# An expert stage in units of two 64-row sub-blocks on raw float32 weights, in place of 128-row blocks on weights split in two

## The reference

```python
def swiglu(h, wg, wu, wd):
    return (jax.nn.silu(h @ wg) * (h @ wu)) @ wd
...
        xs = hp[tok]
        y = swiglu(xs, w_gate_e[e], w_up_e[e], w_down_e[e])
        return (y.astype(jnp.float32) * rw[:, None]).astype(hf.dtype)
```

## Time and profile before

| | |
|---|---|
| median of three runs | 3558.13 us |
| lowest, highest | 3545.75, 3561.34 us |
| span of the profiled execution, first to last instruction | 3472.9 us |
| the profiled execution's own time | not shown; its span is 85.2 us under the median |
| PE, DVE, ACT, POOL busy | 85%, 62%, 49%, 27% of the span |
| mean granted clock of TensorE | 0.935 of full speed |
| moved by DMA | 730.08 MB, mean 210 GB/s |

### The profile page before, as it was taken

How to read it: one execution, slowest core, us unless ns; L and a number is a source line. 1 busy time by engine, 2 the same in 40 slices (tenths; PEclk the granted TensorE clock), 3 DMA queues, 4 the chain that set the end, 5 groups by cost and what they waited for, 6 DMA issues and landing times.

```text
span 3472.9 us, 61999 instructions
## 1 busy us (share of the span) xinstructions
PE 2951.9 (85%) x13151; PEld 2180.6 (63%) x13152; DVE 2164.1 (62%) x3443; ACT 1706.3 (49%) x2435; POOL 925.5 (27%) x794
## 2 busy tenths in 40 slices
PE   6699999999469989888798888888888888998883
PEld 2355555555358877776676767676767667776662
DVE  1146666666643665667676766666766675667774
ACT  0133333333133654656565655556556565656565
POOL 0001111111223333232333333333332323333331
PEclk9899999999779999999899999999999999999896
DMA  9501111111175887989998999899989998899997
GB/s 368 163 25 49 49 48 36 49 36 43 67 182 122 239 228 208 269 260 259 289 295 252 290 281 274 258 271 285 288 259 265 265 293 232 247 266 280 294 275 249
DMA packets 415300, 730.08 MB, mean 210 GB/s; under 512 B 31521, under 2 KB 297377, under 8 KB 414754
## 3 DMA queue, kind: packets, MB, share of 16 engines
q1 hardware_dynamic: 341314, 500.17, 42.5%
q0 software_dynamic: 73824, 228.47, 28.6%
HBM read 587.37 MB, written 141.19 MB: 210 GB/s over the span
## 4 chain that ended last, share of the span: by engine, by line
DMA 45%; PE 22%; issue 12%; DVE 8%; POOL 7%; POOLq 4%; ACT 2%; DVEq 0%; SPq 0%; ACTq 0%
DMA rec<-rec_tab 42%; PE PB L986 8%; POOL arena L461 3%; POOL acc_tab L492 3%; POOLq L476 3%; PE PB L951 2%; PE PB L1068 2%; PE PB L1070 2%; PE PB L1069 2%; DMA arena<-in_ada_b 1%; PE PB L1045 1%; PE PB L956 1%; DMA acc_tab<-arena,rec 1%; PE PB L970 1%; PE PB L1011 1%
## 5 line engine op out<-in xcount | busy, mean ns | idle before, releaser
L887 DVE TENSOR_TENSOR WS<-RAW,WS (+1 forms) x774 | 900.8, 1219 | 127.3 <-ACT WS L586 125.3
L586 ACT CAST WS<-RAW (+1 forms) x774 | 759.5, 1052 | 153.2 <-DMA RAW<-in_w_up_e 99.6
L1068 PE MATMUL PB<-WS,XR 128*128 x1720 | 685.6, 399 | 52.2 <-issue 46.6
L461 POOL DMA_INDIRECT arena<-h_tab,rec x219 | 255.3, 1166 | 1574.7 <-DMA rec<-rec_tab 1381.1
L1070 PE MATMUL PB<-WS,XR 128*128 x1720 | 674.7, 392 | 0.0
L1069 PE MATMUL PB<-WS,XR 128*128 x1720 | 674.0, 392 | 0.0
L917 DVE SCALAR_TENSOR_TENSOR arena<-PB,rec,G 128x512 f32<-128x512 f32 x430 | 302.5, 745 | 383.7 <-DMA acc_tab<-arena,rec 336.5
L1068 PE MATMUL PB<-WS,HR 128*128 x860 | 402.9, 468 | 154.1 <-DVE HR L921 153.0
L492 POOL DMA_INDIRECT acc_tab<-arena,rec x215 | 402.5, 1872 | 93.3 <-issue 68.4
L1068 PEld LDWEIGHTS PB<-WS,XR 128*128 128x128 f32 x1720 | 327.6, 190 | 158.7 <-issue 91.8
L1069 PEld LDWEIGHTS PB<-WS,XR 128*128 128x128 f32 x1720 | 326.7, 190 | 66.1
(11 more groups left out here) (233 smaller groups left out, 2982.6 us busy)
## 6 DMA issues: line engine op xcount, KB each, us to landing
RAW<-in_w_gate_e SPq DMA_DIRECT2D x128, 1024.0 KB
RAW<-in_w_up_e SPq DMA_DIRECT2D x128, 1024.0 KB
RAW<-in_w_down_e SPq DMA_DIRECT2D x128, 1024.0 KB, 8.6
arena<-in_ada_w SPq DMA_DIRECT2D x12, 2048.0 KB, 14.3
arena<-in_x SPq DMA_DIRECT2D x32, 512.0 KB, 3.6
h_tab<-arena SPq DMA_DIRECT2D x17, 512.0 KB, 2.9
acc_tab<-arena SPq DMA_DIRECT2D x16, 512.0 KB, 2.6
out<-fa SPq DMA_DIRECT2D x16, 512.0 KB, 4.7
```

What stands on the lines that cost most here:

```text
L461: g.indirect_dma_start(xg[n % AHEAD], None, h2_tab, bass.IndirectOffsetOnAxis(ap=rec[:, n % UNROLL, 0:1], axis=0)).then_inc(s[f"xg_r{n % A ...
L586: nc.scalar.copy(to, of).then_inc(s["a_hig" if k < 4 else "a_hid"], 1)
L887: last = V.tensor_tensor(lo, raw, hi, ALU.subtract)
L1068: mm(bank, hi[:, k, :], w(k, 0), start=(k == 0), stop=False)
```

## The change

- A unit takes the place of a block: two sub-blocks of 64 rows, which may be of different experts. One lies in columns 0 to 63 of the stationary operand and output partitions 0 to 63, the other in the upper half of both. An expert's rows are padded to a multiple of 64.
- The weights are used as they are, in float32, without a split. Products of the lower half read them from a ring of four slots (`RING`); for the upper half DVE copies gate and up weights (`gu_copy`, 4096 columns, three units ahead) and ACT the down weights (`down_copy`, 2048 columns) into buffers of their own.
- PE's order in an iteration b: gate and up of unit b+1, first column part of the down product of unit b, transposes of the rows of unit b+2 and of the hidden rows of unit b+1, second column part of unit b.
- All records are loaded once, before the stage, by four indirect loads, transposed on PE and kept on chip; POOL loads none in its loop, and DVE copies two columns of them per unit. Padding rows are not fetched.
- A row's depth is stored in another order, so that a weight row of 8 KB per partition can be loaded in one piece. `h2` is written with a stride for it.
- The upper halves add their results to a second copy of the sums, which is zeroed in the row stage by 16 stores on SP's queue, and is loaded and added in the last stage.
- The offsets go from DVE over seven small PE products into `tab`, not over DRAM.

```diff
-SLOTS = 2
+SLOTS = 4
 UNROLL = 8
+SUB = 64
+NSH = T // SUB
+NUNIT = 256
+MAXU = (NSH + T * TOPK // SUB + E) // 2
...
-        RAW = over("RAW", SLOTS * EW, 0)
-        WS = over("WS", 2 * SLOTS * EW, SLOTS * EW, f32r)
-        xg = [arena[:, 36864 + n * D:36864 + (n + 1) * D] for n in range(AHEAD)]
-        XR = over("XR", 2 * D, 40960, f32r)
-        xh, xl = (XR[:, n * D:(n + 1) * D].rearrange("p (k n) -> p k n", k=KD) for n in range(2))
+        RING = arena[:, 0:SLOTS * EW]
+        WBG = [arena[:, 24576 + n * GUW:24576 + (n + 1) * GUW].rearrange("p (a k n) -> p k a n", a=2, k=KD) for n in range(2)]
+        WBD = arena[:, 32768:34816]
+        xg = [arena[:, 34816 + n * D:34816 + (n + 1) * D] for n in range(AHEAD)]
+        xTm = arena[:, 38912:39936].rearrange("p (k n) -> p k n", k=KD)
...
+                if ok(i):
+                    sp.dma_start(acc_tab[bass.ds(i * P + (T + P), P), :], zeros).then_inc(s["z_acc"], 16)
...
+            def gate_up(l, e):
+                at = (l + 3) % SLOTS * EW
+                g = A["w_sh_gate"][0:1] if e is None else A["w_gate_e"][0, bass.ds(e, 1)]
+                u = A["w_sh_up"][0:1] if e is None else A["w_up_e"][0, bass.ds(e, 1)]
+                sp.dma_start(RING[:, at:at + HALF], g.rearrange("a (p k) n -> p (a k n)", p=P)).then_inc(s["w_g"], 16)
+                sp.dma_start(RING[:, at + HALF:at + GUW], u.rearrange("a (p k) n -> p (a k n)", p=P)).then_inc(s["w_u"], 16)
+
+            def down(l, e):
+                at = (l + 3) % SLOTS * EW + GUW
+                d = A["w_sh_down"][0:1] if e is None else A["w_down_e"][0, bass.ds(e, 1)]
+                sp.dma_start(RING[:, at:at + HALF], d.rearrange("a (p k) n -> p (a k n)", p=P)).then_inc(s["w_d"], 16)
...
+            with sp.Fori(1, E // SLOTS) as q:
                 for n in range(SLOTS):
...
+                    e = sp.snap(q * SLOTS + n)
+                    sp.wait_ge(s["w_g"], e * 16 + 16)
...
+                    sp.wait_ge(s["w_u"], e * 16 + 16)
...
+                    u = sp.value_load(tab[0:1, bass.ds(e + (6 * P - 3), 1)], min_val=1, max_val=MAXU)
+                    sp.wait_ge(s["gu_done"], u)
...
+                    gate_up(n + 1, e)
+                    sp.wait_ge(s["w_d"], e * 16)
...
+                    if n == 0:
+                        w = sp.value_load(tab[0:1, bass.ds(e + (6 * P - 4), 1)], min_val=1, max_val=MAXU)
+                    sp.wait_ge(s["y_done"], w)
...
+                    down(n, e - 1)
+                    w = u
...
+                sp.dma_start(fb[:, lo:hi, :], acc_tab[lo * P + T + P:hi * P + T + P, :].rearrange("(t p) n -> p t n", p=P)).then_inc(s[f"f_ib{n}"], 16)
...
+            g.wait_ge(s["p_wo"], NT)
+            g.memset(arena[:, 34816:34816 + AHEAD * D], 0.0).then_inc(s["z_pool"], 1)
 
+            g.wait_ge(s["st_rec"], 16 * TOPK * NT)
+            for c in range(4):
...
+                g.indirect_dma_start(RF[:, c].rearrange("p r a -> p (r a)"), None, rec_sub,
+                                     bass.IndirectOffsetOnAxis(ap=recb[:, c:c + 1], axis=0)).then_inc(s["e_rec"], 16)
+            g.wait_ge(s["z_pool"], 1)
+            g.wait_ge(s["st_h2"], 16 * NT)
+            g.wait_ge(s["v_rec"], AHEAD)
             for n in range(AHEAD):
                 gather(n)
...
-            def load_rec(b, slot):
-                off = g.value_load(tab[0:1, bass.ds(b + 1, 1)],
-                                   min_val=0, max_val=(E + 1) * T - P)
-                g.dma_start(rec[:, slot, :], rec_tab[bass.ds(off, P), :]).then_inc(s["rec_ld"], 16)
-
+            with g.Fori(0, MAXU // UNROLL) as q:
+                with g.If(q * UNROLL < nu):
                     for n in range(UNROLL):
                         b = g.snap(q * UNROLL + n)
-                        with g.If(b < nblk + 1):
+                        with g.If(b < nu):
                             g.wait_ge(s["xg_used"], b + 1)
-                            g.wait_ge(s["rec_ld"], b * 16 + 16 * (AHEAD + 2))
+                            g.wait_ge(s["v_rec"], b + (AHEAD + 1))
                             gather(n + AHEAD)
                             g.wait_ge(s["y_v"], b + 2)
-
                             g.wait_ge(s["added"], b * 16 + 32)
...
-                            g.indirect_dma_start(acc_tab, bass.IndirectOffsetOnAxis(ap=rec[:, (n - 1) % UNROLL, 0:1], axis=0),
-                                                 ys[(n - 1) % 2], None, compute_op=ALU.add).then_inc(s["added"], 16)
-                            load_rec(b + (AHEAD + 2), (n + AHEAD + 2) % UNROLL)
+                            g.indirect_dma_start(acc_tab, bass.IndirectOffsetOnAxis(ap=rec[:, n, 1:2], axis=0),
+                                                 ys[n % 2], None, compute_op=ALU.add).then_inc(s["added"], 16)
...
+            with act.Fori(0, MAXU // UNROLL) as q:
+                with act.If(q * UNROLL < nu):
                     for n in range(UNROLL):
                         b = act.snap(q * UNROLL + n)
...
+                        with act.If(b < nu):
+                            at = act.value_load(tab[0:1, bass.ds(b + (2 * P + 1), 1)], min_val=0, max_val=(SLOTS - 1) * EW)
+                            need = act.value_load(tab[0:1, bass.ds(b + (4 * P + 1), 1)], min_val=16, max_val=16 * (E + 1))
                             act.wait_ge(s["gu_done"], b + 2)
...
+                            silu()
+                            act.wait_ge(s["xg_used"], b + 3)
                             rows_upper()
...
                             act.wait_ge(s["y_done"], b + 1)
...
+                            hidden_T()
+                            act.wait_ge(s["w_d"], need)
...
+                            down_copy(RING[:, bass.ds(act.snap(at + GUW), HALF)])
...
+                    W8(v, "st_h2", 16 * (i - 1))
                     W8(v, "p_h2T", i - 1)
-                    link(V.scalar_tensor_tensor(out=h2, in0=x1, scalar=r2, in1=A2, op0=ALU.mult, op1=ALU.mult))
-                    V.tensor_tensor(h2, h2, B2, ALU.add).then_inc(s["v_h2"], 1)
+                    link(V.scalar_tensor_tensor(out=tmpf, in0=x1, scalar=r2, in1=A2, op0=ALU.mult, op1=ALU.mult))
+                    V.tensor_tensor(h2.rearrange("t (k p) -> t p k", k=KD), tmpf.rearrange("t (p k) -> t p k", k=KD),
+                                    B2.rearrange("t (p k) -> t p k", k=KD), ALU.add).then_inc(s["v_h2"], 1)
...
+            pair = RI[:, :].rearrange("p (a n) -> p n a", a=2)
+            V.tensor_copy(rec[:, 0:5, :], pair[:, 0:5, :]).then_inc(s["v_rec"], 5)
...
+                        with v.If(b < nu):
+                            at = v.value_load(tab[0:1, bass.ds(b + (2 * P + 3), 1)], min_val=0, max_val=(SLOTS - 1) * EW)
+                            need = v.value_load(tab[0:1, bass.ds(b + (4 * P + 3), 1)], min_val=16, max_val=16 * (E + 1))
+                            v.wait_ge(s["eg_done"], b + 2)
+                            gated()
+                            v.wait_ge(s["xg_used"], b + 3)
+                            rows_lower()
                             v.wait_ge(s["y_done"], b + 1)
                             v.wait_ge(s["added"], b * 16 + 16)
...
                             for c in range(2):
...
+                                last_ = V.scalar_tensor_tensor(out=ys[n % 2][:, c * 512:(c + 1) * 512], in0=B[4 + c], scalar=RW[:, bass.ds(b, 1)],
+                                                               in1=G2[:, c * 512:(c + 1) * 512], op0=ALU.mult, op1=ALU.mult)
+                            last_.then_inc(s["y_v"], 1)
+                            V.tensor_copy(rec[:, (n + 5) % UNROLL, :], pair[:, bass.ds(b + 5, 1), :].rearrange("p n a -> p (n a)")).then_inc(s["v_rec"], 1)
+                            v.wait_ge(s["w_g"], need)
...
+                            v.wait_ge(s["w_u"], need)
...
+                            gu_copy(n + 1, RING[:, bass.ds(at, GUW)])
...
+            def gate_up(n, wa):
+
+                for k in range(KD):
+                    mm(B[7][0:SUB, :], xTm[:, k, 0:SUB], wa(k), start=(k == 0), stop=(k == KD - 1))
+                    last = mm(B[7][SUB:P, :], xTm[:, k, SUB:P], WBG[n % 2][:, k], start=(k == 0), stop=(k == KD - 1))
+                last.then_inc(s["gu_done"], 1)
+
+            def down(c, wa):
+
+                for k in range(2):
+                    mm(B[4 + c][0:SUB, :], hT[:, k, 0:SUB], wa(k), start=(k == 0), stop=(k == 1))
+                    last = mm(B[4 + c][SUB:P, :], hT[:, k, SUB:P], WBD[:, k * D + c * 512:k * D + (c + 1) * 512], start=(k == 0), stop=(k == 1))
+                return last
...
+            with pe.Fori(0, MAXU // UNROLL) as q:
+                with pe.If(q * UNROLL < nu):
                     for n in range(UNROLL):
                         b = pe.snap(q * UNROLL + n)
...
+                        with pe.If(b < nu):
+                            at1 = pe.value_load(tab[0:1, bass.ds(b + 1, 1)], min_val=0, max_val=(SLOTS - 1) * EW)
+                            pe.wait_ge(s["v_cg"], b + 2)
```

(13 more changed lines are left out.)

486 lines of the change are left out of this document (220 added, 266 removed).

## The result

The changed kernel takes 3149.5 us (median of four runs, 3141.8 to 3158.7), the kernel before on the same chip 3551.9 (3545.6 to 3561.3): a ratio of 0.886, 95% interval 0.8833 to 0.8886. The forecast was 3300 us with a range from 3220 to 3470, so the direction was right, and the measured time is 150 us under the forecast and 70 under the low end of its range. The profiled execution of the changed kernel ran 3141.75 us with a span of 3139.7: 2 us lie around the span.

What follows compares the result with a forecast made beforehand. POOL's record-load round trip bounds before (11.3 us a block); PE would pace after. Stage 14 + 2088 + 50 = 2152 (-280), rest +29: span 3222, plus 85.2 around it, 3307, given as 3300 us, range 3220 to 3470.

Steps and rivals of the forecast that it cites:

- the three rivals: Expert stage: weights bind (3430 us, chance 0.21); POOL's scatters bind (3410, 0.05); pairs overlap only in part (3776, 0.10).
- scatter 9.6: POOL's loop in the new kernel: wait for the previous scatter 9.0 us plus 0.6 of handover, under the unit's 12.0.
- queues 10.8 to 11.5: DMA per unit: weights 6.3 to 7.0 us plus other queue at most 4.5, fitting narrowly on average under 12.0.
- none of it on the chain: Hi/lo weight splits on ACT and DVE in before: 13 us for each new expert, said not to be on the chain.
- Time around the span: Launch start and end: 85.2 us between span and median of runs, taken as left unchanged and added to span 3222.
- The unit: PE's expert loop: passes 10.34, transposes 1.09, mode changes 0.30, gap 0.20; 11.93, taken as 12.0 us, 2088 for 174 units.
- Stalls for weights: Expert stage: 50 us, between 0 and 200, for clusters of single-sub-block experts that the ring of four does not even out.
- First part: Start of the expert stage: first gate_up and its silu before the loop, 14 us.
- ahead of the stage: Before the expert stage: +3 us for offsets and record loads at its start, +2 for h2's strided write in the row stage.
- The last stage: Tail: 8.4 MB more to load and 16 more additions, +24 us, with the additions under the loads.
- The cover: PE's order: silu and product (1.1 us) hide behind one down part and eight transposes, no stall; without it 190 us.
- The rival of partly overlapping pairs: PE's paired products: each pass costs 0.545 us in place of 0.431, +476 us, 3776 in all; chance 0.10.

Runs made afterwards that it cites:

- the two semaphores alone: Kernel before with record loads alternating between two semaphores, so a gather no longer waits for the load issued just before it: 3327.5 us, ratio 0.952.
- the extra MB: Changed kernel with 1 MB more loaded for each routed expert into a buffer nobody reads: 3251.9 us.
- the last experiments: Changed kernel, last stage: every second of 16 additions moved to POOL, 3134.7 us against 3126.7; DVE's order changed, means ahead of other work, 3146.6 against 3149.3.
- POOL adding: Changed kernel with every second of the last stage's 16 additions on POOL in place of DVE: 3134.7 us against 3126.7.

## Why the prediction was right and where it was wrong

The mechanism was right: the record loop was the wait in front, PE paces the changed kernel, and none of the three rivals came. The time was wrong by three terms of the sum; the largest comes from holding a median of runs against the span of another execution.

**What bounded before, right but not whole.** The round trip of the records was the wait in front: taking it out of before gives 4.8%, putting it into after costs about as much (4.5% to 5.3%). Two readings of it were loose. 8.1 us of landing and 3.5 of issuing are 11.6, not 11.3; and the loop is 11.3 only on average, since the landing is 5.7 us where no weights move. What I missed is how close the other limits stood behind it. I had two of them on paper for the new kernel (scatter 9.6, queues 10.8 to 11.5) and did not ask them of the old one, and I dismissed the splits ("none of it on the chain"), which hold the blocks behind small experts once the loop is gone. That did no harm to the forecast, since a unit of 11.69 us outlasts nearly all of them; it did spoil my forecast for the two semaphores alone. Which part of the change, the longer unit, the four slots or the missing split, carries it past them was not taken apart.

**Time around the span: 83 us, the largest miss, and the step that failed.** "The median of the runs, 3558.1, lies 85.2 over the span, start and end of a launch, which the change leaves." It is 2 us in every run that shows both. The other 83 are time inside the span of a slower execution of before, and the change did not leave them: where before takes over 3550 us the change gains 402 and 410, elsewhere 360 and 375. Where in before they lie stays open, but for some 15 us that the other chip probably explains, ahead of the expert stage. The sum should have ended at 3222 + 2, which is 2.4% over the measured time, or carried the 85 us as an unknown between 2 and 85.

**The unit: 53 us.** Taken as 12.0, measured 11.694. The 24 passes came as worked out (10.30 for 10.34). The rest was put at 1.59 and is 1.39: 0.10 into the transposes (2003.21 to 2003.31), 0.93 and 0.31 for the ten, 0.05 in the first pass after them, and no gap between iterations where I had put 0.20 by the earlier trace rows. Rounding 11.93 up added 0.07 x 174 = 12 us. PE's own time was also better before than I read it: 9.32 us a block, not 9.55, so its work grew by 31 us (174 x 11.694 = 2035 against 215 x 9.32 = 2004), where I had +35 (2088 - 2053); that these agree is luck, as both terms were too high.

**Stalls for weights: 39 us.** Put at 50 between 0 and 200, measured 11. The queues' sum was 10.3 us a unit, under my 10.8 to 11.5, and the extra MB shows what it took to make it bind. That the ring and the copies three units ahead evened out more than I gave them is an argument; no run varied either.

**First part 2 us, ahead of the stage -10.** 11.7 for 14. Ahead of the stage I had +5, measured +15.4. Most of that is not the change's: on the one chip where before and kernels built on the changed one both have a profile, the first product of the expert stage starts at 980.5 in before and at 983.0 and 984.2 in the others, +2.5 and +3.7. **The last stage, -2**, +24 forecast, +25.6 measured; "the additions under the loads" is half true, as the last experiments show. The terms add up: 53 + 39 + 2 - 10 - 2 = 82 us of span and 83 around it; less 7 for rounding 3307 to 3300 and 8 by which the profiled run lay under the median, that is the 150.

**The cover held:** no stall at the hidden rows, none at the row copies, and 1.34 us a unit without it. **DVE's copy** of 4096 columns, bounded by 0 and 4.63, took 2.29 us.

**The rival of partly overlapping pairs is out.** The figure that I set against the trace, from the Trainium skill, page "TensorE: Matmul & The Clock Gate", section "Measured speedup vs the span model", is for three column tiles; carried over to two it would have given 0.546 us for a pass of a pair, an estimate. Measured: 0.43, with or without the second half. The reading of the earlier trace rows that counted entries apart was the right one.

## What to carry to other kernels

When a wait is the whole of a chain, list what else is paid once a block or once an expert (landings, slots, queues, conversions) with its length: taking out the first wait brings you only to the second. Look at the spread of the blocks and not at their mean alone: with two semaphores half of them came within 9.5 us while the mean was 10.65. Fewer blocks, each longer on the busiest engine, should bring you past several such waits at once; this case agrees, but changed other things with it. And hold a trace's sum against a time of the same execution; a median of other runs can be another chip's number.

## What the runs showed of the hardware that was not expected

- Two products on the lower and upper 64 columns of the array, 512 columns each in float32, cost what one costs: 11.687 and 11.693 us a unit without and with the 12 second halves.
- DVE copies float32 from SBUF to SBUF at 0.56 ns an element (2288 ns for 128x4096), where its two-operand work takes 1.13 (4.63 us for the four of the earlier trace rows).
- POOL's issue of a scatter has a median of 1.62 us in before (mean 1.87) and of 2.80 in after. In after 161 of the 174 overlap that copy on DVE (2008.23 to 2010.52, scatter from 2009.17), and the 13 with no work on DVE beside them take 1.58. With POOL adding, DVE's scalings take 11.13 us for 4.87. That it is one cause was not tested.
- TensorE's lower clock is seen behind waits, but not behind every one: in before rounded products start 0.43 us apart behind a wait of 7.64 us (until 2013.78) and 0.23 apart from 2017.9 on (granted clock 0.52 from 2014.0 to 2017.6, then 1.00), and they stay near 0.23 behind a wait of 0.55 us (until 2027.17). In after the passes behind its one stall, of 9.20 us (until 2984.15), start 0.86 us apart and then 0.43 (granted clock 0.50 until 2987.4, then 1.00). The stage's mean clock is 0.95 in before and 1.00 in after, which hardly waits. What the clock costs was not taken apart from the waits themselves.
- A load of 1 KB lands 8.3 us after its issue while weights are loaded and 5.7 us after it while none are (before, windows 1500 to 3300 and 990 to 1150).
- Eight transposes that read every eighth float32 column take 0.06 us more than plain ones.
